# The experts' first three up chunks in the form with high and low inputs side by side

## The chip, the cores and the metric

One core of a Trainium2 chip runs the whole program. The metric is the device time of one launch in microseconds. The kernel before takes 3318.16 us, the median of three runs (3315.14 to 3321.02).

## The reference

Two transformer blocks run one behind the other over 256 tokens of width 2048, all in float32. The change touches the second block's expert layer (`peer`). Each token is projected to queries, the queries are compared with two sets of 128 keys, the 16 best of each are combined, and the 16 best pairs name 16 of 16384 experts per head, with softmax weights over them:

```python
def chunk_fn(args):
    xc, ec, gc = args
    u_sel = jnp.take(peer_u, ec, axis=0)
    h = jnp.einsum("cd,chkd->chk", xc, u_sel)
    a = jax.nn.gelu(h, approximate=False) * gc
    v_sel = jnp.take(peer_v, ec, axis=0)
    return jnp.einsum("chk,chkd->cd", a, v_sel)
```

Since nearly every expert is chosen by some token, the kernel takes all 16384 experts for all tokens: it computes gelu(peer_u x), multiplies it by a dense table of gates (zero where a token has not chosen the expert), and multiplies the result by peer_v.

## The kernel before, in words

**Precision.** Each weight and each activation is split into a high part (a copy to float32r) and a low part (the rest), and a product is the sum of three: high x high, high x low, low x high. The activations of a layer lie in XX, with high and low side by side (XH, XL), or in FH and FL.

**Units.** Weights arrive in units of 128 x 1024 numbers (512 KB) in a ring of five buffers (RAW). ScalarE copies a unit to its high part (HI, four buffers, line 1258, `divide`), VectorE subtracts to get the low part (LO, line 1559), TensorE multiplies (`mm`). The high part of a unit waits until the matmuls of the unit four before it are done; the two splits are queued three units ahead of the matmuls. Each engine works its queue in order.

**Products and pairs.** A product is a group of units that accumulate into one of two pairs of PSUM banks; the next but one product needs the pair again, so it waits until the result has been taken out. `plan()` writes the order of all engines in one list of steps: `product` emits the splits and matmuls of its units, and after each unit `step()` takes the next piece of the lists `evacuations` (results to be taken out), `beside` and `background` (work that goes along).

**The two forms of an up product.** The weights are the stationary operand and the tokens stream through.
- Plain form (lines 1079 to 1081): a unit holds 2 rows of tiles by 512 columns of weights. Per unit there are 24 matmuls of 256 columns: each high tile against XH and against XL, each low tile against XH. Eight units make a product with 512 experts, in two banks.
- Side by side (lines 1049 and 1052, steps `f` and `x`): a unit holds 4 rows of tiles by 256 columns. A high tile meets XX as one operand of 512 columns, so that high x high lands in one half of a bank and high x low in the other; a low tile meets XH alone and adds to the first half. Per unit there are 8 matmuls of 512 columns and 8 of 256. Four units make a product with 256 experts. Afterwards the two halves must be added: ScalarE copies the second halves to SBUF (BF or BP), VectorE adds the first halves out of PSUM (lines 1866 and 1874).

**The expert layer.** There are 8 chunks of 2048 experts. The order is: up 0, 1, 2, then down 1, 0, 2, then up and down of chunks 3 to 7 in turn. Chunks 3 to 7 use the form side by side (`x`, then Gelu in place in SBUF, `hidden`). Chunks 0 to 2 use the plain form (`us`): 12 products of eight units, 96 units in all; ScalarE takes Gelu straight from PSUM (line 1526) to GM2, STAGE and UF.

**What goes along.** While TensorE works on the query projection and the first 50 or so up units, VectorE searches the best keys (`choose`: `best`, `cand0`, `cand1`, `pick0`, `pick1`, `gate`, eight groups of tokens and heads), and ScalarE takes an Exp in each `pick1`. Then comes the step `tables`: six transposes on TensorE behind the 52nd up unit, thirteen small VectorE instructions, the first of which writes KEYS (line 2079). Then 32 blocks of gates follow, about one a unit: `onehot` on VectorE (lines 2104, 2106, 2109: OH, EQ, GOH), `gates_sum` on TensorE (line 1236, 24 small matmuls), `gates_out` on ScalarE. Behind the last block stand `first_mul` (line 2125: chunk 0 times its gates in GM2, then ScalarE copies chunk 2 from UF to GM0, which is UN's memory) and `second_mul` (line 2131: chunk 1 times its gates to HB, ScalarE copies to FH, VectorE writes FL), for four blocks j; the down-projection of chunk 1 starts behind the 96th unit.

Of the kernel before, what the change touches and what calls it, by code (L numbers as in the profile page):

```python
# [66 lines left out]
class Plan:  # L67
# [27 lines left out]
    "onehot": (0, 0, 3), "gates_sum": (1, 0, 0), "gates_out": (0, 2, 0), "gates_side": (1, 0, 2),  # L95
    "us": (0, 2, 0), "first_mul": (0, 1, 1), "second_mul": (0, 1, 2), "third_mul": (0, 0, 1), "split_up": (0, 1, 1),
    "x": (0, 1, 1), "gelu": (0, 2, 0), "weigh": (0, 1, 2), "y": (0, 0, 2),
# [6 lines left out]
    "f": ((DVE_, 1),), "d": ((DVE_, 2),), "dl": ((DVE_, 2),), "h2": ((DVE_, 2),), "q2": ((DVE_, 2),),  # L104
    "o2": ((DVE_, 2),), "o2_last": ((DVE_, 2),), "wq": ((ACT_, 2),), "us": ((ACT_, 2),), "x": ((DVE_, 1),),
    "y": ((DVE_, 2),),
# [8 lines left out]
def plan():  # L115
# [34 lines left out]
    for way, c in order:  # L150
        if way == "down":
            for g in range(4):
                p.units.extend(("peer_v", g, 8 * c + u, 1024) for u in range(8))
        elif c < 3:
            units("peer_ut", range(4 * c, 4 * c + 4))
        else:
            units("peer_ut_rest", range(8 * (c - 3), 8 * (c - 3) + 8))

# [62 lines left out]
    def product(step_, n):  # L221

        pair = pairs[0] % 2
        pairs[0] += 1
        p.pair[step_], p.before[step_], owners[pair] = pair, owners[pair], step_
        p.prior[step_] = latest.get(step_[0])
        latest[step_[0]] = step_
        p.first[step_] = len(p.unit_of)
        both = step_[0] in ("f", "x")
        for u in range(n):  # L230
            if u == (2 if both else 3):
                settle()
# [427 lines left out]
    def first_blocks():  # L660
        for j in range(4):
# [5 lines left out]
            yield  # L667

    def up_staged(c):
        for j in range(4):  # L670
            product(("us", c, j), 8)
            emit("us", c, j)
            staged[c].append(j)

# [43 lines left out]
    for s in p.steps:  # L718
        if s[0] in COUNTS:
# [6 lines left out]
UNITS = {"w_in": 8, "w_out_a": 4, "w_o_attn": 4, "w_mix_out": 8, "ffn_w_up": 4, "w_in_2c": 8, "w_in_2q": 8,  # L726
         "w_in_2kv": 8, "peer_w_q": 8, "peer_ut": 8, "peer_ut_rest": 4}

# [18 lines left out]
def _program(nc, a, out, ctx):  # L747
# [128 lines left out]
    def two(b):  # L876
        return b.rearrange("p (c s) -> p c s", c=2)
# [123 lines left out]
    def tensor(e):  # L1001
# [32 lines left out]
        def unit(i):  # L1034
# [3 lines left out]
            if first:  # L1038
                for s, n in until_taken(step):
                    w.wait_ge(s, n)  # L1040
            if kind in ("f", "x"):
                operand_ready(step, 4 * u + 3)
# [211 lines left out]
    def scalar(e):  # L1254
# [5 lines left out]
        for step in PLAN.steps:  # L1260
# [122 lines left out]
            elif kind == "res1":  # L1383
                g, = k
                w.wait_ge(s_dve, V("mix", 3))
                for t in range(2):
                    w.wait_ge(s_dve, V("res1", g, k=t + 1))
                    if g:
                        w.wait_ge(s_act, A("res1", g - 1, k=t + 1))
                    e.activation(junk1[:, t, :], RES[:, t, 512 * g:512 * g + 512], ACT.Square,  # L1390
                                 accum_out=SSQ[:, t, g:g + 1]).then_inc(s_act, 1)
            elif kind in ("f", "x"):
                if PLAN.prior[step]:
# [112 lines left out]
            elif kind == "gates_out":  # L1506
# [9 lines left out]
                for i in range(2):  # L1516
                    copy(GM[place(2 * r + i)][:, :, 8 * blk - 8:8 * blk + 8],
                         src[:, 16 * i:16 * i + 16, :]).then_inc(s_act, 1)
            elif kind == "us":
                c, j = k  # L1520
                if c == 0:
                    w.wait_ge(s_pe, P("keys", 3))
                w.wait_ge(s_mm, multiplied(step))
                dst = (GM[2], STAGE[:], UF[:])[c]
                for i in range(2):
                    e.activation(dst[:, 4 * j + 2 * i:4 * j + 2 * i + 2, :], two(banks(step)[i]),
                                 ACT.Gelu).then_inc(s_act, 1)
            elif kind == "first_mul":
                j, = k
                w.wait_ge(s_dve, V("first_mul", j))  # L1530
                w.wait_ge(s_act, A("us", 2, j))
                copy(blocks(GM[0], j), blocks(UF, j)).then_inc(s_act, 1)
# [22 lines left out]
    def vector(e):  # L1555
# [103 lines left out]
        for step in PLAN.steps:  # L1659
# [210 lines left out]
            elif kind == "x":  # L1870
# [3 lines left out]
                e.tensor_tensor(HB[:, 2 * k[2]:2 * k[2] + 2, :], halves(step)[:, :, 0, :], BP[:],  # L1874
                                ALU.add).then_inc(s_dve, 1)
            elif kind == "taps1":
                q, i, b = k
# [242 lines left out]
            elif kind == "first_mul":  # L2120
                j, = k
                w.wait_ge(s_act, A("us", 0, j))
                w.wait_ge(s_act, A("gates_out", 0, 31))
                d = blocks(GM[2], j)
                e.tensor_tensor(d, d, blocks(GM[0], j), ALU.mult).then_inc(s_dve, 1)
            elif kind == "second_mul":
                j, = k
                w.wait_ge(s_pe, P("tables"))
                w.wait_ge(s_act, A("us", 1, j))
                w.wait_ge(s_act, A("gates_out", 0, 31))  # L2130
# [84 lines left out]
```

## Time and profile before

| | us |
|---|---|
| median of three runs | 3318.16 |
| lowest, highest | 3315.14, 3321.02 |
| profiled execution, its own time | 3319.9 |
| its span, first to last instruction | 3318.1 |
| TensorE busy | 3264.1 |
| VectorE busy | 2294.6 |
| ScalarE busy | 1549.7 |
| first up unit of chunk 0 to first down unit of chunk 1 | 1801.5 to about 2113 |

Matmuls are pipelined, so a busy TensorE can still have different amounts of work in it; what tells the pace are the starts of its instructions. VectorE's and ScalarE's durations are true ones, but an instruction often starts a little before the recorded end of the one ahead, so the cost to a queue is read from start to start. TensorE's mean granted clock is 0.995 of full speed.

### The profile page before, as it was taken

To read this page: it belongs to the slowest core of one execution; us is meant where nothing else is said; L and a number is where in the kernel's file an instruction comes from. 1 tells how busy PE (TensorE), PEld (TensorE's weight loads), DVE (VectorE), ACT (ScalarE), POOL (GpSimd) and SP (SyncE) were. 2 spreads that over 40 slices of the span, in tenths; PEclk is the share of its full clock that TensorE was granted. 3 is DMA by queue.
4 is the path that set the end of the run, shared out by engine and by line. 5 is a ranking of instruction groups with operands and counts; after the bars stand their busy time and mean duration, and the time that the engine had idled before them with its cause. 6 is when DMAs were issued, how large, how long until landed. Compare 5 with 4: busy or idle time off the path is not lost.

```text
span 3318.1 us, 49691 instructions
## 1 busy us (share of the span) xinstructions
PE 3264.1 (98%) x20978; PEld 2883.9 (87%) x20978; DVE 2294.6 (69%) x3277; ACT 1549.7 (47%) x1987; POOL 5.6 (0%) x14
## 2 busy tenths in 40 slices
PE   9999999999999999998999999999999999999999
PEld 7999998888888888887789999888888888888887
DVE  6765556677577567788659997578787577865554
ACT  4554344555455455555544544444343443434353
POOL 0000000000000000000000000000000000000000
PEclk9999999999999999999999999999999999999999
DMA  7445565656655655552445554554555555555655
GB/s 240 157 148 194 188 207 181 213 180 197 194 180 192 196 189 175 181 167 77 147 154 168 170 174 141 186 171 150 189 172 189 187 183 180 182 185 190 191 189 165
DMA packets 162463, 590.30 MB, mean 178 GB/s; under 512 B 17984, under 2 KB 18144, under 8 KB 161344
## 3 DMA queue, kind: packets, MB, share of 16 engines
q1 hardware_dynamic: 161424, 583.15, 53.2%
q0 software_dynamic: 816, 3.98, 0.4%
q8 instruction: 164, 2.69, 0.3%
q14 instruction: 59, 0.48, 0.0%
HBM read 584.96 MB, written 2.10 MB: 177 GB/s over the span
## 4 chain that ended last, share of the span: by engine, by line
PE 89%; DVE 9%; ACT 2%; issue 1%; DMA 0%; DVEq 0%; ACTq 0%
PE PS L1049 19%; PE PS L1069 12%; PE PS L1071 12%; PE PS L1070 12%; PE PS L1052 10%; PE PS L1079 7%; PE PS L1080 7%; PE PS L1081 7%; DVE LO L1559 3%; PE PS L1236 1%; DVE GB L1968 1%; PE PS L1249 1%; ACT HI L1258 1%; PE PS L1103 0%; ACT UN L1334 0%
## 5 line engine op out<-in xcount | busy, mean ns | idle before, releaser
L1559 DVE TENSOR_TENSOR LO<-RAW,HI 128x1024 fp32r<-128x1024 f32 x1096 | 1327.0, 1218 | 748.1 <-ACT HI L1258 745.7
L1258 ACT ACTIVATE HI<-RAW 128x1024 fp32r<-128x1024 f32 x1096 | 1149.6, 1054 | 1162.2 <-PE PS L1071 596.0
L1049 PE MATMUL PS<-XX,HI 128*128 128x512 f32 x2688 | 735.5, 395 | 0.0
L1069 PE MATMUL PS<-HI,FH 128*128 128x512 f32 x1632 | 644.2, 395 | 5.7 <-DVE FL L1559 5.4
L1071 PE MATMUL PS<-HI,FL 128*128 128x512 f32 x1632 | 637.0, 390 | 0.0
L1070 PE MATMUL PS<-LO,FH 128*128 128x512 f32 x1632 | 635.6, 389 | 0.0
L1079 PE MATMUL PS<-XX,HI 128*128 128x256 f32 x2176 | 625.0, 287 | 9.8 <-DVE LO L1559 9.5
L1080 PE MATMUL PS<-XX,HI 128*128 128x256 f32 x2176 | 617.0, 284 | 0.0
L1081 PE MATMUL PS<-XX,LO 128*128 128x256 f32 x2176 | 616.9, 283 | 0.0
L1049 PEld LDWEIGHTS PS<-XX,HI 128*128 128x128 f32 x2688 | 459.6, 189 | 61.9
L1052 PEld LDWEIGHTS PS<-XX,LO 128*128 128x128 f32 x2688 | 412.4, 189 | 57.2
L1079 PEld LDWEIGHTS PS<-XX,HI 128*128 128x128 f32 x2176 | 418.8, 192 | 17.6 <-DVE LO L1559 13.0
L1052 PE MATMUL PS<-XX,LO 128*128 128x256 f32 x2688 | 427.5, 281 | 0.0
L1080 PEld LDWEIGHTS PS<-XX,HI 128*128 128x128 f32 x2176 | 419.0, 193 | 0.1
L1081 PEld LDWEIGHTS PS<-XX,LO 128*128 128x128 f32 x2176 | 418.7, 192 | 0.0
L1069 PEld LDWEIGHTS PS<-HI,FH 128*128 128x128 f32 x1632 | 306.8, 188 | 69.0 <-issue 7.4
L1071 PEld LDWEIGHTS PS<-HI,FL 128*128 128x128 f32 x1632 | 306.6, 188 | 65.8
L1070 PEld LDWEIGHTS PS<-LO,FH 128*128 128x128 f32 x1632 | 307.0, 188 | 61.7
L2104 DVE TENSOR_TENSOR OH<-KEYS,TAB 128x1024 bf16<-128x1024 bf16 x128 | 87.8, 686 | 22.2 <-PE PS L1236 21.7
L1855 DVE TENSOR_TENSOR RES<-PS,RES 128x512 f32<-128x512 f32 x112 | 72.0, 685 | 21.8 <-PE PS L1071 21.8
L1968 DVE SCALAR_TENSOR_TENSOR GB<-HP,PAR,GB 128x256 f32<-128x256 f32 x180 | 75.7, 478 | 0.0
L2109 DVE TENSOR_TENSOR GOH<-EQ,TG 128x768 bf16<-128x768 bf16 x128 | 71.5, 558 | 4.4
(285 smaller groups left out, 2300.6 us busy)
## 6 DMA issues: line engine op xcount, KB each, us to landing
RAW<-in_peer_v SPq DMA_DIRECT2D x256, 512.0 KB, 3.9
RAW<-in_ffn_w_up SPq DMA_DIRECT2D x176, 512.0 KB, 4.2
RAW<-in_peer_ut_rest SPq DMA_DIRECT2D x160, 512.0 KB, 3.9
RAW<-in_w_in SPq DMA_DIRECT2D x136, 512.0 KB, 4.0
RAW<-in_peer_ut SPq DMA_DIRECT2D x96, 512.0 KB, 3.5
RAW<-in_ffn_w_down SPq DMA_DIRECT2D x88, 512.0 KB, 4.2
RAW<-in_w_mix_out SPq DMA_DIRECT2D x32, 512.0 KB, 4.1
RAW<-in_w_in_2c SPq DMA_DIRECT2D x32, 512.0 KB, 4.0
```

The costliest lines, as they stand in the source:

```text
L1049: e.matmul(o, hi[:, k, x], XX[:, 4 * u + k, :, :].rearrange("p h s -> p (h s)"), start=first and k == 0, stop=False, skip_group_check=True)
L1052: m = e.matmul(o[:, 0:S], lo[:, k, x], XH[:, 4 * u + k, :], start=False, stop=last and k == 3, skip_group_check=True)
L1069: e.matmul(o, x, hi[:, k, :], start=first and k == 0, stop=False, skip_group_check=True)
L1070: e.matmul(o, x, lo[:, k, :], start=False, stop=False, skip_group_check=True)
L1071: m = e.matmul(o, y, hi[:, k, :], start=False, stop=last and k == 1, skip_group_check=True)
L1079: e.matmul(o, h, x, start=first and k == 0 and c % 2 == 0, stop=False, skip_group_check=True)
L1080: e.matmul(o, h, y, start=False, stop=False, skip_group_check=True)
L1081: m = e.matmul(o, l, x, start=False, stop=last and k == 1 and c % 2 == 1, skip_group_check=True)
L1258: return e.activation(dst, src, ACT.Copy) if scale is None else e.activation(dst, src, ACT.Copy, scale=scale)
L1559: return e.tensor_tensor(dst, src, hi.bitcast(F32), ALU.subtract)
L1968: e.scalar_tensor_tensor(out=CV[:, c, :], in0=HP[:, c, j:j + S], scalar=par("cw2", 31 * c + j), in1=CV[:, c, :], op0=ALU.mult, op1=ALU.add ...
L2104: e.tensor_tensor(OH2[:, i], KEYS2[:].unsqueeze(1).to_broadcast([128, 4, 128, 2]), second.to_broadcast([128, 4, 128, 2]), ALU.is_equal).th ...
```

## The change

The steps `us` of the first three chunks take the form side by side. The weights are packed like those of the later chunks (one input `peer_ut` of 32 groups with 4 units each, where there were `peer_ut` and `peer_ut_rest`); the bytes are the same. Each of the 12 products of eight units becomes two of four. Behind each of them ScalarE copies the second halves to BP, and VectorE adds the first halves and writes to GM2, STAGE or UF; behind the second of each two ScalarE takes Gelu in place over 1024 elements (`us_gelu`), queued by `evacuations` behind the next unit's matmuls. `first_mul` and `second_mul` wait for `us_gelu`.

```diff
-    "us": (0, 2, 0), ...
+    "us": (0, 1, 1), "us_gelu": (0, 1, 0), ...
-        both = step_[0] in ("f", "x")
+        both = step_[0] in ("f", "x", "us")
...
+    def up_gelu(c, j):
+        emit("us_gelu", c, j)
+        staged[c].append(j)
+        yield
+
     def up_staged(c):
         for j in range(4):
-            product(("us", c, j), 8)
-            emit("us", c, j)
-            staged[c].append(j)
+            for i in range(2):
+                product(("us", c, j, i), 4)
+            evacuations.append(up_gelu(c, j))
...
-            elif kind == "us":
+            elif kind == "us_gelu":
                 c, j = k
-                if c == 0:
-                    w.wait_ge(s_pe, P("keys", 3))
-                w.wait_ge(s_mm, multiplied(step))
-                dst = (GM[2], STAGE[:], UF[:])[c]
-                for i in range(2):
-                    e.activation(dst[:, 4 * j + 2 * i:4 * j + 2 * i + 2, :], two(banks(step)[i]),
-                                 ACT.Gelu).then_inc(s_act, 1)
+                w.wait_ge(s_dve, V("us", c, j, 1))
+                d = blocks((GM[2], STAGE, UF)[c], j)
+                e.activation(d, d, ACT.Gelu).then_inc(s_act, 1)
...
+            elif kind == "us":
+                c, j, i = k
+                w.wait_ge(s_act, A(*step))
+                if c == 0:
+                    w.wait_ge(s_pe, P("keys", 3))
+                e.tensor_tensor((GM[2], STAGE, UF)[c][:, 4 * j + 2 * i:4 * j + 2 * i + 2, :], halves(step)[:, :, 0, :],
+                                BP[:], ALU.add).then_inc(s_dve, 1)
```

Line numbers in the changed kernel differ by a few: the high part is line 1261, the low part 1558, the tables' first instruction 2085, `first_mul` 2131, `second_mul` 2137.

The queue of ScalarE around the end of the first up product of chunk 0, before (HI is a unit's high part, TK the Exp of the search, GM_99 is GM2):

```order
509 L1258 ACTIVATE HI<-RAW 128x1024 x2
510 L1505 ACTIVATE TK<-TK 128x32
511 L1258 ACTIVATE HI<-RAW 128x1024 x5
512 L1526 ACT_TABLE_LOAD
513 L1526 ACTIVATE GM_99<-PS 128x512 x2
514 L1258 ACTIVATE HI<-RAW 128x1024 x4
```

And the same place after:

```order
510 L1508 ACTIVATE TK<-TK 128x32
511 L1261 ACTIVATE HI<-RAW 128x1024
512 L1261 ACTIVATE BP<-PS 128x512
513 L1261 ACTIVATE HI<-RAW 128x1024 x4
514 L1261 ACTIVATE BP<-PS 128x512
515 L1261 ACTIVATE HI<-RAW 128x1024
516 L1526 ACT_TABLE_LOAD
517 L1526 ACTIVATE GM_99<-GM_99 128x1024
518 L1261 ACTIVATE HI<-RAW 128x1024 x3
```

A pair of Gelus out of PSUM has become a copy after each four units and one Gelu in SBUF, one high part later. The whole queue holds 26 table loads before and after.

The queue of VectorE ahead of the tables step, before (LO is a unit's low part; the rows with 128x2 and the one behind them are the gate step):

```order
1381 L1646 TENSOR_REDUCE TK<-CANE 128x32
1382 L1559 TENSOR_TENSOR LO<-RAW,HI 128x1024 x2
1383 L2072 TENSOR_REDUCE TK<-TK 128x2
1384 L2074 RECIPROCAL TK<-TK 128x2
1385 L2076 TENSOR_TENSOR TK<-TK 128x32
1386 L1559 TENSOR_TENSOR LO<-RAW,HI 128x1024 x3
1387 L2079 CAST KEYS_108<-CONST 128x256
```

After:

```order
1394 L1645 TENSOR_REDUCE TK<-CANE 128x32
1395 L1558 TENSOR_TENSOR LO<-RAW,HI 128x1024
1396 L1880 TENSOR_TENSOR STAGE<-PS,BP 128x512
1397 L1558 TENSOR_TENSOR LO<-RAW,HI 128x1024
1398 L2078 TENSOR_REDUCE TK<-TK 128x2
1399 L2080 RECIPROCAL TK<-TK 128x2
1400 L2082 TENSOR_TENSOR TK<-TK 128x32
1401 L1558 TENSOR_TENSOR LO<-RAW,HI 128x1024 x3
1402 L1880 TENSOR_TENSOR STAGE<-PS,BP 128x512
1403 L2085 CAST KEYS_108<-CONST 128x256
```

The low part at 1395 is that of the 51st up unit. The adds into STAGE at 1396 and 1402 are the twelfth and the thirteenth; the first eight write GM2, and eleven stand ahead of row 1395.

The queue of VectorE behind the last block of gates, before (GM_99 by UN is `first_mul`, HB and FL `second_mul`):

```order
1524 L2125 TENSOR_TENSOR GM_99<-GM_99,UN 128x1024
1525 L1559 TENSOR_TENSOR LO<-RAW,HI 128x1024
1526 L2131 TENSOR_TENSOR HB<-STAGE,GM_98 128x1024
1527 L1559 TENSOR_TENSOR FL<-HB,FH 128x1024
1528 L2125 TENSOR_TENSOR GM_99<-GM_99,UN 128x1024
1529 L1559 TENSOR_TENSOR LO<-RAW,HI 128x1024
1530 L2131 TENSOR_TENSOR HB<-STAGE,GM_98 128x1024
1531 L1559 TENSOR_TENSOR FL<-HB,FH 128x1024
1532 L1559 TENSOR_TENSOR LO<-RAW,HI 128x1024 x6
```

After:

```order
1550 L2137 TENSOR_TENSOR HB<-STAGE,GM_98 128x1024
1551 L1558 TENSOR_TENSOR FL<-HB,FH 128x1024
1552 L2131 TENSOR_TENSOR GM_99<-GM_99,UN 128x1024
1553 L1558 TENSOR_TENSOR LO<-RAW,HI 128x1024
1554 L2137 TENSOR_TENSOR HB<-STAGE,GM_98 128x1024
1555 L1558 TENSOR_TENSOR FL<-HB,FH 128x1024
1556 L1558 TENSOR_TENSOR LO<-RAW,HI 128x1024
1557 L1880 TENSOR_TENSOR UF<-PS,BP 128x512
1558 L1558 TENSOR_TENSOR LO<-RAW,HI 128x1024 x4
```

The two rounds of `first_mul` and `second_mul` stand as before; the next add comes behind the low part that follows them.

## Rows read from the trace of the kernel before

**Rows 1.** The page, parts 1 and 4: busy time by engine, and the chain.
```profile
PE 3264.1 (98%) x20978; PEld 2883.9 (87%) x20978; DVE 2294.6 (69%) x3277; ACT 1549.7 (47%) x1987; POOL 5.6 (0%) x14
...
PE 89%; DVE 9%; ACT 2%; issue 1%; DMA 0%; DVEq 0%; ACTq 0%
```

**Rows 2.** Busy time in stretches: length, PE, PEld, DVE, ACT, POOL, clock, DMA.
```profile
1801.50:1873.00 71.50, 71.50 (x599) 71.50 (x598) 67.84 (x198) 36.61 (x41) 0.00 (x0) 1.00 0.52 166
1873.00:1954.00 81.00, 76.99 (x624) 75.10 (x623) 77.38 (x226) 39.37 (x44) 0.00 (x0) 1.00 0.51 169
...
1971.00:2066.00 95.00, 95.00 (x1340) 93.88 (x1336) 72.83 (x114) 38.97 (x62) 0.00 (x0) 1.00 0.45 149
2066.00:2084.00 18.00, 14.89 (x127) 14.48 (x123) 10.73 (x10) 9.24 (x11) 0.00 (x0) 1.00 0.25 88
```

**Rows 3.** Waits of TensorE, 1782 to 1975: total us, times, longest.
```profile
PE PS L1079 <- DVE LO L1559: 3.7, 5, 0.9
```

**Rows 4.** Waits of VectorE, 1782 to 1954.
```profile
DVE LO L1559 <- ACT HI L1258: 0.5, 1, 0.5
```

**Rows 5.** TensorE in order of time, old form: start, us, instruction.
```profile
1770.00 0.28 PE L1080 MATMUL PS<-XX,HI 128*128 128x256 f32 x1
1770.12 0.28 PE L1081 MATMUL PS<-XX,LO 128*128 128x256 f32 x1
```

**Rows 6.** TensorE in order of time, the form of the later chunks.
```profile
2441.84 1.09 PE L1049 MATMUL PS<-XX,HI 128*128 128x512 f32 x4
...
2443.24 1.09 PE L1049 MATMUL PS<-XX,HI 128*128 128x512 f32 x4
```

**Rows 7.** ScalarE in order of time, first chunk (idle time before in brackets).
```profile
1812.22 1.06 ACT L1258 ACTIVATE HI<-RAW 128x1024 fp32r<-128x1024 f32 x1 [1.70 <-PE PS L1081]
1815.10 1.06 ACT L1258 ACTIVATE HI<-RAW 128x1024 fp32r<-128x1024 f32 x1 [1.82 <-PE PS L1081]
```

**Rows 8.** ScalarE in order of time, fourth chunk.
```profile
2440.64 0.60 ACT L1258 ACTIVATE BP<-PS 128x512 f32<-128x512 f32 x1 [1.97 <-PE PS L1052]
```

**Rows 9.** VectorE in order of time, first chunk.
```profile
1815.06 1.22 DVE L1559 TENSOR_TENSOR LO<-RAW,HI 128x1024 fp32r<-128x1024 f32 x1
1816.19 0.18 DVE L2072 TENSOR_REDUCE TK<-TK 128x2 f32<-128x32 f32 x1
...
1828.63 1.23 DVE L1559 TENSOR_TENSOR LO<-RAW,HI 128x1024 fp32r<-128x1024 f32 x1 [0.46 <-ACT HI L1258]
```

**Rows 10.** VectorE in order of time, fourth chunk.
```profile
2442.55 0.68 DVE L1874 TENSOR_TENSOR HB<-PS,BP 128x512 f32<-128x512 f32 x1
2443.15 1.22 DVE L1559 TENSOR_TENSOR LO<-RAW,HI 128x1024 fp32r<-128x1024 f32 x1
```

**Rows 11.** Groups by line and shape, VectorE, 2415 to 3250: the adds.
```profile
L1874 DVE TENSOR_TENSOR HB<-PS,BP 128x512 f32<-128x512 f32 x40 | 27.6, 691 | 34.0 <-ACT BP L1258 34.0
```

**Rows 12.** VectorE in order of time, up to the tables step.
```profile
1952.37 2.35 DVE L1559 TENSOR_TENSOR LO<-RAW,HI 128x1024 fp32r<-128x1024 f32 x2
...
1960.34 0.29 DVE L2079 CAST KEYS<-CONST 128x256 bf16<-128x256 f32 x1 [1.16 <-PE PS L1224]
```

**Rows 13.** TensorE in order of time, tables step and first gates.
```profile
1959.48 0.82 PE L1224 MATMUL PS<-CONST,TK 128*128 128x128 f32 x6
...
1970.69 0.77 PE L1236 MATMUL PS<-GOH,OH 128*128 128x32 bf16 x24 [0.45 <-DVE GOH L2109]
...
1974.25 0.77 PE L1236 MATMUL PS<-GOH,OH 128*128 128x32 bf16 x24
...
1977.82 0.77 PE L1236 MATMUL PS<-GOH,OH 128*128 128x32 bf16 x24
```

**Rows 14.** VectorE in order of time, after the last gates.
```profile
2066.88 1.22 DVE L2125 TENSOR_TENSOR GM<-GM,UN 128x1024 f32<-128x1024 f32 x1 [1.58 <-ACT GM L1258]
```

**Rows 15.** TensorE in order of time: its last two waits.
```profile
2079.38 0.38 PE L1079 MATMUL PS<-XX,HI 128*128 128x256 f32 x1 [1.62 <-DVE LO L1559]
...
2083.99 0.38 PE L1079 MATMUL PS<-XX,HI 128*128 128x256 f32 x1 [1.49 <-DVE LO L1559]
```

More of the change, by code:

```diff
@@ L95 @@
     "onehot": (0, 0, 3), "gates_sum": (1, 0, 0), "gates_out": (0, 2, 0), "gates_side": (1, 0, 2),
-    "us": (0, 2, 0), "first_mul": (0, 1, 1), "second_mul": (0, 1, 2), "third_mul": (0, 0, 1), "split_up": (0, 1, 1),
+    "us": (0, 1, 1), "us_gelu": (0, 1, 0), "first_mul": (0, 1, 1), "second_mul": (0, 1, 2), "third_mul": (0, 0, 1), "split_up": (0, 1, 1),
     "x": (0, 1, 1), "gelu": (0, 2, 0), "weigh": (0, 1, 2), "y": (0, 0, 2),
@@ L104 @@
     "f": ((DVE_, 1),), "d": ((DVE_, 2),), "dl": ((DVE_, 2),), "h2": ((DVE_, 2),), "q2": ((DVE_, 2),),
-    "o2": ((DVE_, 2),), "o2_last": ((DVE_, 2),), "wq": ((ACT_, 2),), "us": ((ACT_, 2),), "x": ((DVE_, 1),),
+    "o2": ((DVE_, 2),), "o2_last": ((DVE_, 2),), "wq": ((ACT_, 2),), "us": ((DVE_, 1),), "x": ((DVE_, 1),),
     "y": ((DVE_, 2),),
@@ L153, in plan @@
                 p.units.extend(("peer_v", g, 8 * c + u, 1024) for u in range(8))
-        elif c < 3:
-            units("peer_ut", range(4 * c, 4 * c + 4))
         else:
-            units("peer_ut_rest", range(8 * (c - 3), 8 * (c - 3) + 8))
+            units("peer_ut", range(8 * c, 8 * c + 8))
     landed, divided = [0], [0]
@@ L726 @@
 UNITS = {"w_in": 8, "w_out_a": 4, "w_o_attn": 4, "w_mix_out": 8, "ffn_w_up": 4, "w_in_2c": 8, "w_in_2q": 8,
-         "w_in_2kv": 8, "peer_w_q": 8, "peer_ut": 8, "peer_ut_rest": 4}
+         "w_in_2kv": 8, "peer_w_q": 8, "peer_ut": 4}
 class Waits:
@@ L1040, in unit @@
                     w.wait_ge(s, n)
-            if kind in ("f", "x"):
+            if kind in ("f", "x", "us"):
                 operand_ready(step, 4 * u + 3)
@@ L1391, in scalar @@
                                  accum_out=SSQ[:, t, g:g + 1]).then_inc(s_act, 1)
-            elif kind in ("f", "x"):
+            elif kind in ("f", "x", "us"):
                 if PLAN.prior[step]:
@@ L1530, in scalar @@
                 w.wait_ge(s_dve, V("first_mul", j))
-                w.wait_ge(s_act, A("us", 2, j))
+                w.wait_ge(s_act, A("us_gelu", 2, j))
                 copy(blocks(GM[0], j), blocks(UF, j)).then_inc(s_act, 1)
@@ L2121, in vector @@
                 j, = k
-                w.wait_ge(s_act, A("us", 0, j))
+                w.wait_ge(s_act, A("us_gelu", 0, j))
                 w.wait_ge(s_act, A("gates_out", 0, 31))
@@ L2128, in vector @@
                 w.wait_ge(s_pe, P("tables"))
-                w.wait_ge(s_act, A("us", 1, j))
+                w.wait_ge(s_act, A("us_gelu", 1, j))
                 w.wait_ge(s_act, A("gates_out", 0, 31))
@@ L2200 @@
         "keys": g["peer_sub_keys_2"].transpose(3, 0, 1, 2).reshape(128, 16, 128),
-        "peer_ut": _units(g["peer_u_2"][:6144].T),
-        "peer_ut_rest": _units(g["peer_u_2"][6144:].T, 256, 4),
+        "peer_ut": _units(g["peer_u_2"].T, 256, 4),
         "peer_v": _units(g["peer_v_2"]),
```

## The prediction

> **What bounds the kernel now.** I read the page's engine line and chain first [rows 1]: TensorE is busy 98% of the span and holds 89% of the chain that ended last, VectorE 9%. The next question is where the 9% lies, so I took the busy times of stretches of the up-projection of the first three chunks [rows 2]. From 1801.5 to 1954 us VectorE is busy 145.2 of 152.5 us (67.84 and 77.38), which with its small gaps between instructions is no rest at all: over 1782 to 1954 it waited once, for 0.5 us [rows 4]. In the same time ScalarE is idle for half. TensorE at first keeps up, because the splits into high and low parts run three units ahead; then that lead is used up and it waits for VectorE's low parts, 3.7 us in 5 waits [rows 3]. So in this stretch the order and the sum of VectorE's instructions set the end (each unit's low part, 1.13 us from its start to the next instruction [rows 9], and the search for the best keys between them). From 1971 to 2066 us it is turned round: TensorE is busy 95.00 of 95.00 us, VectorE 72.83. From 2066 to 2084 neither is full (14.89 and 10.73 of 18): two waits of TensorE for low parts, 1.62 and 1.49 us, at the end of a chain of round trips between VectorE and ScalarE that starts with the product at 2066.88 [rows 14, 15]. After 2084 TensorE runs alone again.
>
> **What the change does to TensorE.** A unit of 512 KB was 24 matmuls of 256 columns, started 0.12 us apart [rows 5]: 2.88 us, and the high-part copies of ScalarE follow at that pace (1812.22 to 1815.10) [rows 7]. In the new form it is 8 matmuls of 512 and 8 of 256 columns. The chunks from the fourth on have this form already: half a unit takes 2443.24 - 2441.84 = 1.40 us [rows 6], so a unit takes 2.81. That is 0.07 us a unit, and 96 units would give 6.7 us if TensorE set the pace throughout. The columns streamed are the same, 6144; only the number of matmuls falls, from 24 to 16.
>
> By the Trainium skill (TensorE: Matmul & The Clock Gate, Back-to-back issue gap) an isolated matmul at full clock costs its columns at 2.4 GHz plus about 2.5 ns; an estimate from that page is 2.62 us for the old unit and 2.60 for the new one, a gain of 0.02. The trace does not agree with either size (0.12 us for 256 columns, where the page would have 0.109), and the sum goes by the trace; with the page's figures TensorE would give back 0.7 us where I take 2.6, and the result would be 2 us later.
>
> **What it does to ScalarE.** Twelve pairs of Gelu out of PSUM become 24 copies of 0.60 us [rows 8] and 12 Gelu of 1024 elements (about the 1.06 us of a copy of that size [rows 7]), some 14 us more in 310. It is idle half the time in the saturated stretch [rows 2], and the number of table loads stays. A Gelu now waits for VectorE's add and holds ScalarE's next high part behind it. Between the add and the low part that needs that high part, VectorE has another low part (1.13) and mostly one or two steps of the search (some 1.7 us each: at 2.88 a unit, 1.13 of it the low part), 2.8 us or more, against Gelu and copy, 2.1; so I cost it at nothing. It also gives something: VectorE's one wait before 1954, 0.46 us at 1828.63 [rows 9], comes from a high part queued behind the first Gelu pair; the copy that replaces it is half as long and no table load stands ahead of it, so that wait goes.
>
> **What it does to VectorE.** It gets 24 adds out of PSUM, 0.68 us each, of which the next instruction sees 0.60 (2442.55 to 2443.15) [rows 10]. Thirteen stand ahead of the tables step. The low part of the 51st up unit (the first of the two at 1952.37 [rows 12]), for which TensorE waits, is queued behind eleven of them; the twelfth follows it and meets a lead that has come back (two low parts and the gate's three small instructions are all that is left of the search there). The thirteenth is immediately in front of the tables.
> - Path to the low part of the 51st unit: 11 x 0.60 = +6.6, less the wait of 0.46: **+6.1 us**. A faster TensorE gives nothing here, it only waits longer. The lead that hid the deficit before 1873 is used up earlier, by the same sum.
> - Units 51 and 52 run back to back: -0.14. Then the tables step. Its transposes begin at 1959.48 [rows 13] and VectorE's first instruction came at 1960.34, after a wait of 1.16 [rows 12]. Now the copy (0.60) must end, then the add (0.60), about 1.3 us after the last matmul instead of 0.7: **+0.6**. It is seen by TensorE, which stood 0.45 us at 1970.69 for the third one-hot block [rows 13], the end of that same sequence.
> - From there to the last block of gates TensorE is the bound: 26 units (the 56th to the 81st) at 3.57 us with a block of gates in them (1974.25 to 1977.82 [rows 13]) become 3.50: **-1.8 us**. VectorE's share of such a unit is 72.83 of 95.00 [rows 2], 2.74 us, and a quarter of an add makes it 2.9, so it keeps up.
> - 2066 to 2084: the chain of round trips is counted from the last gates, and no add stands in it (the next one, for the product that ends with the 84th unit, is queued behind the low part at which the chain ends; TensorE waits for the 86th and 87th units' low parts, at 2079.38 and 2083.99 [rows 15]). So these five units win nothing: 0. The last ten win 0.07 each: **-0.7 us**. In the last product the round trip copy, add, Gelu is about 1.4 us longer than the Gelu alone; the lead of the following down units, over 2 us, takes it.
>
> Sum: 6.1 - 0.1 + 0.6 - 1.8 - 0.7 = **+4.1 us**. The profiled execution took 3319.9 us (span 3318.1), which gives 3324.0; it is 1.7 above the median of the three runs, 3318.16, and against that the forecast is **3322.3 us**. Bounds: an add costs between 0.60 and its full 0.69, +1.2 at most over thirteen; none of a new wait of ScalarE up to 0.5 us at three places, +1.5; the tail between keeping its units' gain and one add in the chain, -0.4 to +0.7. An own range of 3319 to 3326.
>
> **Rivals.**
> - *TensorE sets the pace everywhere.* For it: weight loads fill 71.50 of 71.50 us from 1801.5 to 1873 while VectorE has 67.84 [rows 2]. Against it: TensorE's waits for low parts [rows 3], and VectorE without a wait for 170 us [rows 4]. The adds would be covered, 96 x 0.07 = 6.7 us less: 3311.4. The Trainium skill (Perfetto Trace Analysis, Identifying the Most-Contended Engine) judges TensorE by its share of weight loads and other engines by occupancy, and calls the highest the one to improve; by this rule the stretch belongs to TensorE, and dropping a third of its weight loads is right. The rows of waits speak against it here. 8%.
> - *VectorE stands before each add.* The slow side, one mechanism: the add is queued in order and waits for ScalarE's copy out of the same product. In the later chunks VectorE stood 34.0 us for 40 adds, 0.85 us each [rows 11]. If it does so in the saturated stretch too, thirteen cost 11 us more: 3333.4. It decides where VectorE reaches the add less than 0.6 us after the product's last matmul. At the first product that matmul ends at about 1815.05 and a copy would end at 1815.70 (1815.10 + 0.60 [rows 7, 8]); VectorE is busy with a low part until 1816.19 to 1816.28 [rows 9]. That is half a microsecond to spare, and more later, as VectorE falls behind. 12%.
> - *The adds fit into VectorE's small gaps.* It is busy 145.2 of 152.5 us, so 7 us are gaps between dependent small instructions; if an add could stand in them the 6.6 us go and only TensorE's gain stays: 3318.2 - 2.6 = 3315.6. Against it: the queue is in order, and no instruction was seen to fill such a gap. 10%.
> - The forecast itself: 70%.
>
> **How the numbers follow.** Changes under 0.2%, 6.6 us, can't be told from none with this kernel. Faster by more than that is the first rival alone, 0.08. Slower by more is over 3324.8: the second rival, 0.12, and the upper part of the forecast's own range, 0.13 of 0.70. The rest, 0.67, is the same. The range leaves out the first rival and about the far end of the second: 3314 to 3331.
>
> **What would show it.** In the trace after: TensorE's units at 2.81 where nothing is waited for, 3.50 with gates. Its waits for low parts before the tables step go from 3.7 to about 13 us (6.1 more for the later low part, and 3.5 that 50 faster units leave it to wait), and they begin earlier. VectorE's wait for the copy stays below 2 us before the tables step; if it is 10, the second rival holds. The tables step begins some 6.7 us later than 1960.34, the last gates end some 4.8 later than before, the down-projection of the second chunk starts some 4 us later. If the tables step is no later than before, the forecast is wrong and one of the fast rivals holds; if the down-projection is later by much more than 4, the tail has taken up an add.

## The result

The changed kernel takes 3323.95 us, the median of 16 runs (3319.39 to 3326.25), beside 3316.78 for 16 runs of the kernel before (3315.14 to 3321.02). The ratio is 1.0016, with an interval of 1.0009 to 1.0023: slower by 5.3 us, 3.0 to 7.6. It is taken over all runs and is not the ratio of the two medians. The forecast was +4.1 (3322.3 us against the 3318.16 of three runs), a ratio of 1.0012. The times of both kernels fall into two groups, and the medians happen to lie in different ones (7.2 us apart). The medians of the lower groups (3319.4 to 3320.8 after, 3315.1 to 3318.4 before) are 3.5 us apart, those of the upper groups 5.1. In the table further down, one execution of e1 of 6323.93 us is left out of its median and ratio.

The profiled execution took 3324.8 us (span 3323.0) against 3319.9 (3318.1). These lines of the page after answer to [rows 1]:

```profile
PE 3258.9 (98%) x20210; PEld 2842.4 (86%) x20210; DVE 2309.0 (69%) x3301; ACT 1560.2 (47%) x1999; POOL 5.6 (0%) x14
...
PE 86%; DVE 11%; ACT 2%; issue 1%; DMA 0%; SPq 0%; DVEq 0%; ACTq 0%
```

TensorE has 768 matmuls and 5.2 us of busy time less, VectorE 24 instructions and 14.4 us more, and VectorE's share of the chain has risen from 9 to 11%.

Two rows of TensorE bound the stage that the change touches, the first matmul of the first up unit and the first of the down-projection. Before (start, us, instruction):

```profile
1801.54 0.28 PE L1079 MATMUL PS<-XX,HI 128*128 128x256 f32 x1
...
2112.88 0.40 PE L1069 MATMUL PS<-HI,FH 128*128 128x512 f32 x1
```

After:

```profile
1802.51 1.09 PE L1052 MATMUL PS<-XX,HI 128*128 128x512 f32 x4
...
2117.79 0.40 PE L1072 MATMUL PS<-HI,FH 128*128 128x512 f32 x1
```

The stage has gone from 311.34 to 315.28 us, +3.94. After it both executions run another 1205.2 us. The remaining 0.97 of the span's 4.9 lies ahead of the first up unit, in code that is the same in both: between 30 and 50 us the granted clock was 0.91 before and 0.83 after. In the traces of this study the first up unit begins anywhere from 1795.3 to 1802.5 us, so I compare stages and not spans.

The busy time in stretches after, answering to [rows 2] (length, PE, PEld, DVE, ACT, POOL, clock, DMA):

```profile
1802.50:1873.00 70.50, 68.22 (x389) 59.01 (x388) 67.47 (x193) 36.77 (x42) 0.00 (x0) 1.00 0.52 160
1873.00:1961.00 88.00, 79.18 (x432) 66.89 (x431) 84.21 (x242) 41.61 (x46) 0.00 (x0) 1.00 0.54 162
1978.00:2072.00 94.00, 93.79 (x1138) 83.55 (x1139) 77.35 (x122) 42.87 (x67) 0.00 (x0) 1.00 0.50 152
2072.00:2090.00 18.00, 14.50 (x82) 12.35 (x81) 11.09 (x10) 9.43 (x12) 0.00 (x0) 1.00 0.26 86
```

Up to 1961 us VectorE is busy 151.68 of 158.5 us, the same 95 to 96% as before. TensorE has dropped from 95 to 90% in the second stretch and weight loads from 75 of 81 to 67 of 88, and nothing came of it. The waits tell the same. TensorE's, 1782 to 1985 (answering to [rows 3]):

```profile
PE PS L1052 <- DVE LO L1558: 10.9, 16, 1.7
PE PS L1239 <- DVE GOH L2115: 1.1, 2, 0.8
```

VectorE's, 1782 to 1980 ([rows 4] had one before the tables step; now both lie just ahead of it, none before 1962):

```profile
DVE STAGE L1880 <- ACT BP L1261: 0.4, 1, 0.4
DVE LO L1558 <- ACT HI L1261: 0.4, 1, 0.4
```

### The profile page after: what moved, and what is told of

It is laid out like the page before. It is cut to its first block, busy times and chain, and to the rows that moved or that the text cites. A ratio compares the mean times of both kernels' runs of the same rounds, so it can differ in the third digit from the quotient of the medians.

```text
span 3323.0 us, 48198 instructions
## 1 busy us (share of the span) xinstructions
PE 3258.9 (98%) x20210; PEld 2842.4 (86%) x20210; DVE 2309.0 (69%) x3301; ACT 1560.2 (47%) x1999; POOL 5.6 (0%) x14
## 4 chain that ended last, share of the span: by engine, by line
PE 86%; DVE 11%; ACT 2%; issue 1%; DMA 0%; SPq 0%; DVEq 0%; ACTq 0%
PE PS L1052 21%; PE PS L1072 12%; PE PS L1074 12%; PE PS L1073 12%; PE PS L1055 11%; PE PS L1082 5%; PE PS L1083 5%; PE PS L1084 5%; DVE LO L1558 3%; PE PS L1239 1%; DVE GB L1974 1%; PE PS L1252 1%; ACT HI L1261 1%; DVE TK L1604 1%; DVE TK L1610 1%
## 5 line engine op out<-in xcount | busy, mean ns | idle before, releaser
L1052 PE MATMUL PS<-XX,HI 128*128 128x512 f32 x3456 | 949.6, 396 | 14.6 <-DVE LO L1558 14.4
L1052 PEld LDWEIGHTS PS<-XX,HI 128*128 128x128 f32 x3456 | 590.3, 189 | 97.8 <-DVE LO L1558 18.9
L1055 PEld LDWEIGHTS PS<-XX,LO 128*128 128x128 f32 x3456 | 530.0, 189 | 73.7
L1055 PE MATMUL PS<-XX,LO 128*128 128x256 f32 x3456 | 549.5, 281 | 0.0
L1082 PE MATMUL PS<-XX,HI 128*128 128x256 f32 x1408 | 404.1, 287 | 2.7 <-DVE LO L1558 2.6
L1083 PE MATMUL PS<-XX,HI 128*128 128x256 f32 x1408 | 399.7, 284 | 0.0
L1084 PE MATMUL PS<-XX,LO 128*128 128x256 f32 x1408 | 399.5, 284 | 0.0
L1082 PEld LDWEIGHTS PS<-XX,HI 128*128 128x128 f32 x1408 | 271.5, 193 | 8.1 <-issue 3.9
L1083 PEld LDWEIGHTS PS<-XX,HI 128*128 128x128 f32 x1408 | 271.7, 193 | 0.1
L1084 PEld LDWEIGHTS PS<-XX,LO 128*128 128x128 f32 x1408 | 271.5, 193 | 0.0
L1261 ACT ACTIVATE BP<-PS 128x512 f32<-128x512 f32 x64 | 38.3, 598 | 110.0 <-PE PS L1055 110.0
```

What stands on the lines that cost most here:

```text
L1052: e.matmul(o, hi[:, k, x], XX[:, 4 * u + k, :, :].rearrange("p h s -> p (h s)"), start=first and k == 0, stop=False, skip_group_check=True)
L1055: m = e.matmul(o[:, 0:S], lo[:, k, x], XH[:, 4 * u + k, :], start=False, stop=last and k == 3, skip_group_check=True)
L1082: e.matmul(o, h, x, start=first and k == 0 and c % 2 == 0, stop=False, skip_group_check=True)
L1083: e.matmul(o, h, y, start=False, stop=False, skip_group_check=True)
L1084: m = e.matmul(o, l, x, start=False, stop=last and k == 1 and c % 2 == 1, skip_group_check=True)
L1261: return e.activation(dst, src, ACT.Copy) if scale is None else e.activation(dst, src, ACT.Copy, scale=scale)
```

## The experiments

Each is read by its stage, since the median of a run carries what happens ahead of it too. "Sum" is the difference of the stage and of what follows it against the kernel before, in one trace each; the last column is the difference of the medians on the same chip.

| kernel | stage | expected | sum | ratio, interval | median less before |
|---|---|---|---|---|---|
| before | 311.34 | | | | |
| after | 315.28 | 315.4 | +4.0 | 1.0016, 1.0009 to 1.0023 | +7.2 |
| e1 late | 308.77 | 308.8 | -2.6 | 0.999, 0.9981 to 0.9998 | -2.5 |
| e2 early | 317.67 | 317.9 | +6.3 | 1.0019, 1.001 to 1.0028 | +6.3 |
| e3 double | 322.30 | 323.1 | +10.9 | 1.0029, 1.0018 to 1.0041 | +11.3 |
| e4 adds alone | 317.39 | 317.4 | +6.0 | 1.0019, 1.001 to 1.0028 | +7.5 |
| e5 GpSimd | 317.69 | 308.3 | +7.1 | 1.0022, 1.0013 to 1.0031 | +6.8 |
| e6 slower search, before | 305.36 | 306.3 | -5.2 | 0.9987, 0.9978 to 0.9997 | -3.1 |
| e7 slower search, after | 307.88 | 305 | -2.7 | 0.9996, 0.9987 to 1.0005 | -0.6 |
| e8 GpSimd, slower search | 311.77 | 300 | +2.0 | 1.0005, 0.9996 to 1.0014 | +2.8 |
| e9 late, slower search | 305.01 | 303.6 | -5.5 | 0.9984, 0.9975 to 0.9993 | -5.4 |
| e10 still slower search, after | 309.91 | 304 | -0.7 | 0.9998, 0.9989 to 1.0007 | 0.0 |
| e11 short Gelu | 315.23 | 315.3 | +3.9 | one run | |

**e1, the form for the last 40 up units alone.** Products (0, 0) to (1, 2) keep the plain form:

```diff
+            if (c, j) in PLAIN:
+                product(("up", c, j), 8)
+                emit("up", c, j)
+                staged[c].append(j)
+                continue
             for i in range(2):
                 product(("us", c, j, i), 4)
```

> Only the last five groups of 512 experts (chunk 1 group 3 and all of chunk 2, the 57th to the 96th up unit) take the form side by side; the first 56 units keep the plain form, so no add stands in VectorE's saturated stretch. The up stage (start of the first up unit's matmuls to start of the first down unit's) lasts 311.3 us before and 315.3 with the whole change. Theory (VectorE sets the end before the tables step, TensorE behind it): 25 units with gates and the last 10 win 0.07 us each, 311.3 - 2.5 = 308.8 us, and the time is 2.5 us below before. Rival (an add costs about 0.3 us wherever it stands, net of the faster units): +1.7 us, 313.0.

The stage is 308.77: 2.6 us faster than before, and the whole kernel 0.999 of it. Up to the tables step nothing moves (VectorE's first instruction of it comes 158.8 us after the first up unit, in both); TensorE's waits before it:

```profile
PE PS L1092 <- DVE LO L1577: 3.7, 5, 0.9
PE PS L1249 <- DVE GOH L2134: 0.4, 1, 0.4
```

These 3.7 us in 5 waits are those of [rows 3]. The whole gain comes behind, where TensorE sets the pace.

**e2, the other half.** The same edit with `PLAIN` naming (1, 3) to (2, 3), so that the first 56 units take the form.

> The other half of the change: the first 56 up units take the form side by side, the last 40 keep the plain form. Theory: +6.1 at the 51st unit, -0.1, +0.6 at the tables step and nothing given back, 311.3 + 6.6 = 317.9 us for the up stage, some 6.6 us above before in the time. Rival that TensorE sets the pace: 56 x 0.07 less, 307.4. The two halves together should add up to the whole change (+6.6 - 2.5 = +4.1).

The stage is 317.67, +6.3. With e1's -2.6 that gives +3.8 where the whole change has +3.9: the two halves add up, one loses on VectorE and the other wins on TensorE.

**e3, thirteen adds made twice.**

```diff
+                if (c, j, i) <= (1, 2, 0):
+                    e.tensor_tensor(UF[:, 2 * i:2 * i + 2, :], halves(step)[:, :, 0, :], BP[:], ALU.add)
```

> The whole change, and the first thirteen adds are made twice, the first time into memory that is not used yet (UF). Theory: each further add costs its 0.60 us from start to start, also the one in front of the tables step: 13 x 0.60 = 7.8 us more than the change, up stage 323.1. If the cost of the change came from VectorE's wait for the copy and not from the add's own time, the second add would come free of a wait and fill time that was lost: under 2 us more.

The stage grew by another 7.0 us over after, 0.54 an add: each add goes through to the end nearly whole. It is 0.8 us less than expected; one cause is to be seen, since VectorE's wait of 0.4 for the copy ahead of the tables step has gone under the longer queue.

**e4, the adds alone in the kernel before.** Thirteen adds of the same size, two inputs in SBUF, wait for nothing, one in each fourth unit:

```diff
+            if step_[0] == "us" and u % 4 == 3 and extra[0] < 13:
+                emit("extra", extra[0])
+                extra[0] += 1
```

> The kernel before, matmuls unchanged, with thirteen adds of 128x512 in SBUF put into VectorE's queue where the change puts its first thirteen, waiting for nothing. Theory: the first eleven cost 0.60 each less the one wait of 0.46 that they fill, +6.1; the thirteenth waits for no copy and lies in the 1.16 us in which VectorE waits for the tables' transposes, so +0. Up stage 317.4 us, 6.1 above before. Rival that the adds fit into small gaps or that TensorE sets the pace: 311.3.

317.39 as expected, +6.05 without any change to TensorE or ScalarE. So it is the length of VectorE's queue that costs, not the copies, not the table loads, not the new waits. Against this kernel after is 2.1 us shorter, which is about TensorE's 2.6 less what it pays at the tables step.

**e11, the round trip of Gelu.** Gelu runs over 8 elements instead of 1024, so the up outputs go on nearly all without it:

```diff
-                e.activation(d, d, ACT.Gelu).then_inc(s_act, 1)
+                e.activation(d[:, 0:1, 0:8], d[:, 0:1, 0:8], ACT.Gelu).then_inc(s_act, 1)
```

> The changed kernel with each Gelu of the first three chunks cut to 8 of its 1024 elements (the rest keeps the sum without Gelu): the round trip from VectorE's add to ScalarE stays, its length goes from 1.06 us to some 0.2. Theory: it is hidden behind VectorE's own queue before the tables step, up stage 315.3, at most 0.5 less. Rival that the round trip of Gelu holds the high parts up: 12 x up to 0.8 us less, 306 to 312.

315.23 against 315.28, and the tables' first instruction comes 165.3 us after the first up unit in both. So the time for which Gelu holds ScalarE costs nothing. Its wait for the add is still there in this kernel; that it costs nothing ahead of the tables step is shown by after itself, where VectorE waits for no high part before 1962 us.

**e5, the add on GpSimd.** ScalarE copies both halves, GpSimd adds them in SBUF; VectorE gets nothing new:

```diff
+            elif kind == "us":
+                c, j, i = k
+                w.wait_ge(s_act, A(*step))
+                d = (GM[2], STAGE, UF)[c][:, 4 * j + 2 * i:4 * j + 2 * i + 2, :]
+                e.tensor_tensor(d, d, BP[:], ALU.add).then_inc(s_pool, 1)
```

> The whole change in form, but VectorE makes no add: ScalarE copies both halves out of PSUM (BP and the destination) and GpSimd, idle before, adds them in SBUF. Theory: VectorE's queue before the tables step is that of before, so TensorE waits for it as before; the wait of 0.46 goes, and the faster units count from the tables step on: 311.3 - 0.5 - 1.8 - 0.7 = 308.3 us for the up stage, 3 below before. Rival: GpSimd's adds slow VectorE's own instructions while both work in SBUF; then the low parts (1.22 us) and the search get longer and the stage is above 311.

A miss for the theory; what I had put down as the rival holds. The stage is 317.69, worse than after, though VectorE has no add in its queue. The groups by line and shape of this kernel, VectorE over a stretch with 55 low parts that ends ahead of the tables step (count, busy, mean ns of one, idle):

```profile
L1576 DVE TENSOR_TENSOR LO<-RAW,HI 128x1024 fp32r<-128x1024 f32 x55 | 69.6, 1273 | 0.0
...
L1626 DVE MAX8 TK<-SUB 128x8 f32<-128x128 f32 x24 | 7.1, 295 | 0.8
...
L1641 DVE TENSOR_TENSOR GB<-TK 128x256 f32<-128x256 f32 x12 | 6.1, 507 | 0.0
```

And the same groups of the kernel before, over its 55:

```profile
L1559 DVE TENSOR_TENSOR LO<-RAW,HI 128x1024 fp32r<-128x1024 f32 x55 | 66.2, 1209 | 0.5 <-ACT HI L1258 0.5
...
L1609 DVE MAX8 TK<-SUB 128x8 f32<-128x128 f32 x24 | 7.1, 295 | 0.8
...
L1624 DVE TENSOR_TENSOR GB<-TK 128x256 f32<-128x256 f32 x12 | 5.0, 418 | 0.0
```

Some kinds are longer, MAX8 is not. The single instructions show why. GpSimd, in order of time:

```profile
1833.87 1.67 POOL L1003 TENSOR_TENSOR GM<-GM,BP 128x512 f32<-128x512 f32 x1 [9.86 <-ACT GM L1268]
1846.26 1.30 POOL L1003 TENSOR_TENSOR GM<-GM,BP 128x512 f32<-128x512 f32 x1 [10.72 <-ACT GM L1268]
...
1952.58 2.03 POOL L1003 TENSOR_TENSOR STAGE<-STAGE,BP 128x512 f32<-128x512 f32 x1 [14.44 <-ACT STAGE L1268]
```

VectorE at the same times:

```profile
1833.18 1.21 DVE L1576 TENSOR_TENSOR LO<-RAW,HI 128x1024 fp32r<-128x1024 f32 x1
1834.30 1.29 DVE L2080 TENSOR_TENSOR TK<-TK 128x32 f32<-128x32 f32 x1
...
1846.27 0.29 DVE L1626 MAX8 TK<-SUB 128x8 f32<-128x128 f32 x1
1846.60 0.09 DVE L1628 MATCH_VALUE_LOAD TK<-TK,SUB 128x8 f32 x1
1846.68 0.28 DVE L1628 FIND_INDEX8 TK<-TK,SUB 128x8 uint32<-128x128 f32 x1
1846.88 1.76 DVE L1576 TENSOR_TENSOR LO<-RAW,HI 128x1024 fp32r<-128x1024 f32 x1
...
1953.39 1.26 DVE L1651 TENSOR_SCALAR TK<-TK 128x32 uint32<-128x32 uint32 x1
```

The 128x32 operation, 0.18 us elsewhere, took 1.29 and ended at 1835.59; GpSimd's add ended at 1835.54. The low part begun at 1846.88 took 1.76 instead of 1.21, that is 0.55 more, and GpSimd ended 0.68 after it began. MAX8 and FIND_INDEX8 ran through GpSimd's add at their usual length, and so did MATCH_REPLACE8, TENSOR_REDUCE and RECIPROCAL wherever they met one. It is not only operations with two inputs that stood still: the TENSOR_SCALAR at 1953.39, with one, took 1.26 us instead of 0.17, and a CAST at 1925.16 took 1.18 instead of 0.18. So each add on GpSimd (1.30 us undisturbed, 1.4 to 1.5 in the mean) holds up certain operations of VectorE until it is done, and is itself held by one that runs (1.67 and 2.03 above).

From the first add to the tables step there are twelve adds on GpSimd, and eleven instructions of VectorE are longer than usual, by 9.1 us together. That is 0.76 an add, where an add in VectorE's own queue costs 0.60, and the tables' first instruction comes 167.3 us after the first up unit, against 165.3 in after and 158.8 before. This is the exclusive lock on the shared port pair that the Trainium skill describes (SBUF — State Buffer, SBUF: two separate sides): held for the whole instruction, between a GpSimd operation that reads SBUF and a VectorE operation with two SBUF inputs or in a 2-port mode. For the operations with two inputs the trace agrees with it in kind and in time; whether the TENSOR_SCALAR and the CAST ran in such a mode no run here shows. My theory had left the lock out, and the rival had it without a price.

**e6 to e10, a slower search.** VectorE is full up to the tables step because the search is spread over 50 units; after it there is room (77.35 of 94 us). The pieces of search a unit go from 0.9 to 0.8, and those of gates from 1.15 to 1.6 so that they end in time. In e10 the 0.8 is 0.75.

```diff
-    rate[0] = 0.9
+    rate[0] = 0.8
...
-        rate[0] = 1.15
+        rate[0] = 1.6
```

The edit in the kernel before (e6):

> The kernel before with the key search spread over more units (a step of it after 0.8 of the units' turns instead of 0.9), and the gates at 1.6 blocks a unit instead of 1.15 so that they end at the same unit. A group of the search is 17.4 us of VectorE; with ten low parts of 1.13 it needs 28.7 us where TensorE takes 28.8 for ten units. Theory: TensorE no longer waits for low parts ahead of the tables step, 311.3 - 5 = 306.3 us for the up stage. If something else than VectorE's sum set the end there, the stage stays at 311.

In the kernel after (e7):

> The changed kernel with the same spreading. VectorE needs 17.4 + 10 x (1.13 + 0.15) = 30.2 us for ten units that take TensorE 28.1, over 58 units 12 us of deficit against a lead of 7: some 5 us of waits. Theory: up stage about 305 us, one below the plain form with the same spreading, where with the old spreading it was 4 above. Rival that the adds cost the same wherever VectorE has room: still 4 above, 310.

In e5's kernel (e8):

> The add on GpSimd and the search spread, both. VectorE 28.7 us for ten units of 28.1: the lead of 7 us takes the deficit of 3.5 over 58 units. Theory: no waits for low parts before the tables step, up stage 306.3 - 6.7 + 0.5 = about 300 us, 11 below before, the full gain of the form. If GpSimd slows VectorE, between 300 and 308.

In e1's kernel (e9):

> The form side by side only for the last 40 up units (as in the run of the late half), and the search spread over more units as in the two runs before (0.8, gates 1.6). Theory: from the 305.4 us of the plain form with this spreading, 25 units with gates and the last 9 win 0.07 each, 2.4, and one add now stands in the chain of round trips behind the gates, +0.6: up stage 303.6 us, about 7.7 below before. Rival: the waits for the one-hot blocks behind the tables step eat the gain, 305 or more.

The kernel after with 0.75 (e10):

> The whole change with the search spread further (0.75; gates 1.6 blocks a unit, which now end five units later). With 0.8 VectorE fell short by about 2.7 us for ten units. At 0.75 a group covers 10.7 units: 18 + 10.7 x 1.28 = 31.7 us of VectorE against 30.0, 1.7 short, over six groups 10 against a lead of 7. Theory: waits for low parts before the tables step fall from 4.4 to about 1 to 2 us and the up stage from 307.9 to about 304. Rival that the adds cost something else than VectorE's time: no gain, 308.

e6 gains 6.0 us of stage: TensorE waits for no low part before the tables step any more. Of this 0.8 is lost again behind the stage, in e7, e9 and e10 too: some 95 us into the down-projections TensorE waits 1.3 us for a block of gates, where the kernel before waits 0.5. e9 has the lowest time of all, 3310.48 us, 0.9984 of before (0.9975 to 0.9993); but its stage is only 0.35 under e6's and 1.4 over the expectation. e7 came out 3 us over what I expected. Its waits of TensorE, 1782 to 1985:

```profile
PE PS L1052 <- DVE LO L1558: 4.4, 6, 0.9
PE PS L1239 <- DVE GOH L2115: 2.5, 1, 2.5
```

From 1797 to 1960 us VectorE is still busy 154.36 of 163: with the adds, 0.8 is not slow enough. e10 shows that slower isn't the way out either. Its waits before 1990 fell, to 2.5 us where I expected 1 to 2, and those for low parts behind grew from e7's 2.2 to 5.5; the one-hot blocks cost no more than in e7 (2.5 and 1.4). First 1782 to 1990, then 1990 to 2210:

```profile
PE PS L1052 <- DVE LO L1558: 2.5, 4, 0.8
```

```profile
PE PS L1052 <- DVE LO L1558: 5.5, 3, 3.3
PE PS L1239 <- DVE GOH L2115: 3.6, 2, 2.2
```

The last gates now end 278.3 us into the stage, against 264.6 in e7, so `first_mul` and `second_mul` come late too. In their chain VectorE has low parts only every 7.9 us (2079.44, 2087.36, 2095.28), where a unit takes TensorE 2.81, and TensorE waits 1.94 and 3.30 us for the last two of them. e9 and e7 also show an add inside the chain of round trips behind the gates, which the prediction had kept free of one. VectorE in e9, in order of time:

```profile
2068.46 1.23 DVE L1577 TENSOR_TENSOR LO<-RAW,HI 128x1024 fp32r<-128x1024 f32 x1 [2.08 <-ACT HI L1271]
2069.60 0.68 DVE L1899 TENSOR_TENSOR UF<-PS,BP 128x512 f32<-128x512 f32 x1
2070.20 1.22 DVE L2156 TENSOR_TENSOR HB<-STAGE,GM 128x1024 f32<-128x1024 f32 x1
```

TensorE waited 2.15 us for the low part at the chain's end, where e6, without an add there, has a wait of 1.2: more than the add's 0.60, in part since the shorter units let TensorE arrive sooner. TensorE behind that wait:

```profile
2074.96 1.65 PE L1062 MATMUL PS<-XX,HI 128*128 128x512 f32 x4 [2.15 <-DVE LO L1577]
...
2077.26 1.84 PE L1062 MATMUL PS<-XX,HI 128*128 128x512 f32 x4
...
2079.41 1.08 PE L1062 MATMUL PS<-XX,HI 128*128 128x512 f32 x4
```

The unit took 2079.41 - 2074.96 = 4.45 us instead of 2.81, 1.6 more, at a granted clock of 0.66 from 2075 to 2080 us. The next low part was done by about 2076.1, and TensorE waits for no other up to the down-projection, so nothing hides this. Behind e6's wait of 1.2 the clock stayed at 1.00. That is enough to account for the 1.4 us over the expectation; the rival, which put it on the one-hot blocks, has the number right (305) and the cause wrong, since TensorE's wait for them is 2.5 us here and 2.4 in e6. An execution of e9 in which the clock stays up is not on record.

e8 missed by 12 us, and lies above the 308 that its expectation gave as the worst case too: the 300 left out GpSimd's hold on VectorE, and the bound had it too small. VectorE's longer instructions up to the tables step sum to 10.5 us (TensorE's waits for low parts before it are 6.3 us in 9).

## Why the prediction was right

By its own steps; shifts are against the kernel before, less the 0.97 us by which the stage began later.

| step | forecast | measured, from rows |
|---|---|---|
| low part of the 51st up unit | +6.1 | 1959.45 - 1952.37 - 0.97 = +6.11 |
| first instruction of the tables step | +6.6 | 1967.86 - 1960.34 - 0.97 = +6.55 |
| last block of gates | +4.8 | 2071.01 - 2065.38 - 0.97 = +4.66 |
| first down unit | +4.1 | 2117.79 - 2112.88 - 0.97 = +3.94 |

The rows of after for it, VectorE up to the tables step (answering to [rows 12]):

```profile
1959.45 1.22 DVE L1558 TENSOR_TENSOR LO<-RAW,HI 128x1024 fp32r<-128x1024 f32 x1
1960.58 0.68 DVE L1880 TENSOR_TENSOR STAGE<-PS,BP 128x512 f32<-128x512 f32 x1
1961.18 1.21 DVE L1558 TENSOR_TENSOR LO<-RAW,HI 128x1024 fp32r<-128x1024 f32 x1
...
1967.25 0.69 DVE L1880 TENSOR_TENSOR STAGE<-PS,BP 128x512 f32<-128x512 f32 x1 [0.42 <-ACT BP L1261]
1967.86 0.28 DVE L2085 CAST KEYS<-CONST 128x256 bf16<-128x256 f32 x1
```

and TensorE's gates, where two neighbouring starts give the unit (answering to [rows 13]), and the waits behind them (answering to [rows 15]):

```profile
1966.43 0.82 PE L1227 MATMUL PS<-CONST,TK 128*128 128x128 f32 x6
...
1981.71 0.77 PE L1239 MATMUL PS<-GOH,OH 128*128 128x32 bf16 x24
1985.21 0.77 PE L1239 MATMUL PS<-GOH,OH 128*128 128x32 bf16 x24
...
2071.01 0.77 PE L1239 MATMUL PS<-GOH,OH 128*128 128x32 bf16 x24
...
2085.01 1.19 PE L1052 MATMUL PS<-XX,HI 128*128 128x512 f32 x4 [1.94 <-DVE LO L1558]
...
2089.63 1.20 PE L1052 MATMUL PS<-XX,HI 128*128 128x512 f32 x4 [1.56 <-DVE LO L1558]
```

- *Eleven adds, 6.1.* The add takes 0.60 of the queue: 1960.58 to 1961.18. e3 and e4 confirm the place and the size, with 0.54 for each further add and the whole loss from adds alone. VectorE's wait of 0.46 [rows 9] is gone.
- *Tables step, +0.6.* The transposes start 1966.43 - 1959.48 - 0.97 = 5.98 later, the tables' first instruction 6.55: +0.57.
- *26 units with gates, -1.8.* 1985.21 - 1981.71 = 3.50 us each, as forecast; the shift goes down from 6.55 to 4.66 by the last block, -1.9.
- *The tail, 0 and -0.7.* From the last gates to the down units -0.72. The two waits are 1.94 and 1.56, where they were 1.62 and 1.49: the shorter units turned into wait, as a chain on other engines makes them.
- *ScalarE, nothing.* Shown for Gelu by e11, which takes nearly all of it away and leaves the stage, and for the copies by e4, where the adds without them cost 6.05.
- *Waits of about 13 us.* The view has 10.9. It counts from the recorded end of a matmul, which lies 0.16 us behind the start of its successor (1.09 for a group whose successor starts after 0.93), so 16 waits hide 2.6 us and the five before hid 0.8. With these it is 13.5 and 4.5, a growth of 9.0 where 9.6 was forecast.

*TensorE sets the pace* has fallen: weight loads went from all of the first stretch to 59.01 of 70.50 us without gain. From the tables step on TensorE does set it, and e1 gained 2.6 us there. The Trainium skill's rule that spoke for this rival (Perfetto Trace Analysis, Identifying the Most-Contended Engine) named the wrong engine in the first stretch; the waits named the right one. *VectorE stands before each add* has fallen too: of the thirteen adds one waited, 0.42 us. The first had more room than I gave it, 1815.71 + 0.60 for the copy against 1817.19 for the add, since at 2.81 a unit the copy comes earlier. *Adds in small gaps* is refuted by e3 and e4. Against the first rival the prediction also says that VectorE ran without a wait for 170 us; [rows 4] has one of 0.5, which its own sum uses.

The prediction held that a change under 0.2% can't be told from none. With 16 runs of each kernel the interval is 0.07% to either side, so the 0.16% is a slowdown, not noise.

What stays open: the ratio says +5.3 us and the stage +3.9. The difference lies within the interval, and upstream of the stage these executions differ by several us without any change; whether 1 us of it belongs to the change was not settled.

## What to carry to other kernels

When one engine is full in one stretch and another in the next, price a trade between them per stretch: the same edit cost 6.3 us in the first 56 units and gained 2.6 in the last 40, and applying it to those 40 alone turned a loss into a gain. The waits of the bounding engine say where the border is; the shares of busy time alone, of weight loads above all, do not. Before a job is handed to an idle engine, look at what it shares with the full one: moved to GpSimd, an add cost VectorE 0.76 us, more than the 0.60 of doing it itself.

## What was not expected of the hardware

- GpSimd's add of 128x512 float32 in SBUF takes 1.30 us undisturbed against 0.68 for VectorE's out of PSUM. In that time VectorE's TENSOR_TENSOR with both inputs in SBUF stood still (1.29 us for one of 0.18), and so did a TENSOR_SCALAR and a CAST with one (1.26 and 1.18 us for 0.17 and 0.18), while MAX8, FIND_INDEX8, MATCH_REPLACE8, TENSOR_REDUCE and RECIPROCAL ran.
- TensorE's clock after a wait. In e11 this unit followed a wait of 1.94 us, and four matmuls that take 1.09 took 2.08:

```profile
2080.08 2.08 PE L1052 MATMUL PS<-XX,HI 128*128 128x512 f32 x4 [1.94 <-DVE LO L1558]
```

The stretches around it (columns as above):

```profile
2070.00:2080.00 10.00, 8.13 (x47) 6.93 (x45) 5.93 (x6) 3.91 (x4) 0.00 (x0) 1.00 0.18 52
2080.00:2084.00 4.00, 3.92 (x12) 3.37 (x13) 2.88 (x4) 2.81 (x4) 0.00 (x0) 0.57 0.46 131
2084.00:2090.00 6.00, 6.00 (x34) 5.06 (x34) 5.71 (x6) 3.58 (x4) 0.00 (x0) 1.00 0.62 180
```

A granted clock of 0.57 is nearly all at the lower level, 1.2 GHz. In after the same wait of 1.94 was followed by 1.00:

```profile
2085.00:2089.00 4.00, 3.06 (x16) 2.51 (x16) 2.87 (x3) 2.88 (x4) 0.00 (x0) 1.00 0.38 131
```

It cost nothing in e11, because the next low part would have been waited for anyway: the second wait, 1.56 in after, is missing there. In e7 (0.72 behind a wait of 2.2) and e9 (0.66, 2.15) the drop came too, and no wait followed to hide it: the unit took 4.40 and 4.45 us instead of 2.81. In e7 that is 1.6 of the 2.9 us by which it missed. In e10 (0.70 from 2090 to 2100, behind waits of 1.94 and 3.3) the drop behind the first wait was hidden by the second. How long TensorE waited does not tell whether the clock falls: behind a wait for one-hot blocks of 2.4 us it was 0.79 in e6 (1984 to 1992), behind one of 2.5 us 1.00 in e7 (1984 to 1996).
